# Splitting the first layer's input and the first two weight slabs on ScalarE and VectorE, with GpSimd beginning at the third slab

## The chip, the cores and the metric

The kernel runs on one core of a Trainium2 chip. The metric is the device time of one execution, in microseconds (us). A core has a matrix engine (TensorE, PE in the rows; its weight loads are PEld), VectorE (DVE), ScalarE (ACT), GpSimd (POOL) and SyncE, which here only issues DMAs (SPq). The engines run their own instruction streams and meet at semaphores.

## What is computed

Two layers of a decoder trunk over 528 tokens (16 meta tokens and 512 others) of 1024 channels. The part that matters here is the very start of the first layer: a root mean square norm and the first projection.

```python
def rms_norm(t, g, eps=NORM_EPS):
    y = t32 * lax.rsqrt(jnp.mean(t32 * t32, axis=-1, keepdims=True) + eps)
    return (y * g)
...
    for l in range(DEPTH):
        u = rms_norm(h, norm_mix[l])
        proj = u @ w_in[l]
        glu_in, q, k, v, gates = jnp.split(proj, SPLITS, axis=-1)
        a = glu_in + b_glu[l]
        a = a[..., :C_CONV] * jax.nn.sigmoid(a[..., C_CONV:])
        a = causal_depthwise_conv(a, conv_w[l], conv_b[l])
        ...
        h = h + merged @ w_o[l]
        u = rms_norm(h, norm_mlp[l])
        h = h + jnp.square(jax.nn.relu(u @ w_up[l])) @ w_down[l]
```

The kernel multiplies the input by the gain before the projection and applies the inverse root afterwards, so the projection needs only `h * gain`, while the inverse root needs the sum of the squares of `h` over all channels.

## The kernel before

Channels lie on the 128 partitions: `h` is 8 tiles of 128 x 528. Every float32 product is made of three products of parts: an operand is split into a high part (rounded to the type fp32r) and a low part (the rest), and TensorE adds high x high, high x low and low x high. So the input tile `u[:, 0, i]` is the high part of `h * gain`, `u[:, 1, i]` the low part, and a slab of weights `w_raw` (128 x 2048 float32, 1 MB) becomes `w_hi` and `w_lo`. There are two buffers of each; slabs alternate between them.

The start of layer 0 runs as follows.

SyncE issues the transfers: `h` tiles 0 and 1, slab 0, `h` tiles 2 and 3, 4 and 5, 6 and 7, three small constants (L468, semaphore `in_landed`), slab 1 (L469). The transfer of slab 2 waits until slab 0 has been split (`w_ready`), that of slab 3 until slab 1 has.

GpSimd splits each slab in `split` (L493 to L496): a tiny `tick`, one TENSOR_SCALAR over 128 x 2048 for `w_hi`, four TENSOR_TENSOR over 128 x 512 for `w_lo`, then `w_ready`. From slab 2 on it first waits until TensorE has finished the slab that was in the buffer (`w_used`).

ScalarE and VectorE go through the 8 input tiles in `norm_tile`. ScalarE writes the square into one of two buffers (L828) and the high part (L830). VectorE adds the square to `sumsq` (L1074) and writes the low part (L1075), then raises `u_ready`. ScalarE waits before tile k for the VectorE work on tile k - 2.

TensorE waits for the small constants and for slab 0, then runs the first output tile: 8 input chunks with 6 matmuls of 264 columns each (L588), each chunk waiting for `u_ready`. Between the first and second output tile it sums `sumsq` over partitions (`partition_sums`, L622 and L625). Then come the second tile of slab 0, both tiles of slab 1, and so on; each slab is two output tiles of 48 matmuls. The fourth output tile reuses the PSUM of the second and so waits (`a_free`) for VectorE's L1269, which needs the inverse root: L1244, a square root on ScalarE (L968), the reciprocal L1246, and three instructions of a Newton step (L1081 to L1083).

Order on each engine is the written order; there is no planner around this place.

Of the kernel before, what the change touches and what calls it, by code (L numbers as in the profile page):

```python
# [25 lines left out]
ACT = mybir.ActivationFunctionType  # L26
# [201 lines left out]
def build(nc, x_t, w_slabs, pvecs, rows_in, ident_in, mask_in, identb_in, out, h_spill):  # L228
    ctx = ExitStack()
    with ctx:  # L230
# [8 lines left out]
        def at(name, shape, dt, offset):  # L239
            return nc.alloc_sbuf_tensor_at(name, shape, dt, offset=offset)  # L240
# [11 lines left out]
        down_tmp = at("down_tmp", [P, T], F32, r_x)  # L252
        sumsq = at("sumsq", [P, T], F32, r_x + ROW)
        sq = at("sq", [P, 2, T], F32, r_x + 2 * ROW)

        o_t = at("o_t", [P, NT, T], F32, r_o)
        glu_g = at("glu_g", [P, 2, T], F32, r_o)
# [85 lines left out]
        const_ready = sem("const_ready")  # L343
        h_new = sem("h_new")
        u_hi, u_ready = sem("u_hi"), sem("u_ready")
        ms_ready, sqrt_ready = sem("ms_ready"), sem("sqrt_ready")
        ln_ready = sem("ln_ready")
        glu_sig, glu_out = sem("glu_sig"), sem("glu_out")
# [134 lines left out]
        def _(pool):  # L483
            chain = Count(pool, p_chain)

            def split(b, nth, first=False):

                pool.wait_ge(w_landed[b], 16 * nth + 16)
                if not first:

                    pool.wait_ge(w_used, 2 * nth + (b - 1))

                nc.gpsimd.tensor_tensor(tick[:], ones[:, 0:1], ones[:, 0:1], ALU.mult)  # L493
                chain.link(nc.gpsimd.tensor_scalar(w_hi[:, b, :], w_raw[:, b, :], 1.0, 1.0, ALU.mult, ALU.mult))  # L494
                for c in range(0, SLAB, SLAB // 4):
                    last = nc.gpsimd.tensor_tensor(w_lo[:, b, c:c + SLAB // 4], w_raw[:, b, c:c + SLAB // 4], w_hi[:, b, c:c + SLAB // 4], ALU.subtract)  # L496
                last.then_inc(w_ready, 1)
# [51 lines left out]
                nc.gpsimd.tensor_tensor(t4[:, :, :, H2:HD], x4[:, :, :, 0:H2], mid4(tabs[:, x, 1, :, H2:HD], 4), ALU.mult).then_inc(turned, 1)  # L549

            pool.wait_ge(const_ready, 1)
            for b in range(2):
                split(b, 0, first=True)
            done = 1
            for layer in range(LAYERS):
                s0 = layer * SLABS + S_QKV
# [19 lines left out]
        def _(pe):  # L576
# [183 lines left out]
            for layer in range(LAYERS):  # L760

                a_slabs(layer, 0, A_GLU, N_GLU // 2, u, (u_ready, layer * 2 * NT), full=True,
                        hooks=[lambda: partition_sums(layer, u_ready, (layer * 2 + 1) * NT, sumsq, full=True, cols=True)])

                pe.wait_ge(a_free[0], layer * A_TILES // 2 + NT)
                for stage in range(5):
                    tiles, n = b_tiles(layer), b_before(layer, stage)
                    for step, x, *c in schedule(layer, stage):
                        if step == "tile":
                            what, t = tiles[x]  # L770
                            slab = layer * SLABS + S_QKV + 3 * stage + "vqk".index(what)
                            pe.wait_ge(w_ready, slab + 1)
                            b_tile(layer, n + x, slab % 2, t, c[0])
                        elif step == "gate":
                            early_gate(layer, x, c[0])
                        elif step in ("q", "k"):
                            qk_transposes(layer, x, step, c[0] if c else None)
                        elif step == "s":
                            if (x, *c) == (0, 0):
                                pe.wait_ge(a_free[1], layer * A_TILES // 2 + NT)  # L780
                            scores(layer, x, c[0])
                        elif step == "t":
                            transposes(layer, x, c[0])
                        elif step == "pv":
                            values(layer, x)
                        elif step == "y":
                            y_transposes(layer, x)

                pe.wait_ge(exp_done, (layer + 1) * HEADS * 2 * 3)
                pe.wait_ge(a_free[1], (layer * A_TILES + A_GATE + EARLY_GATES) // 2)  # L790


                channel_sums(layer, ln_ready, layer + 1, [r_inv2[:], conv[:, NT - 1, :]], st_full)

                def last_y():

                    pe.wait_ge(centred, layer * NT + 1)
                    y_transposes(layer, HEADS - 1)
                def squares_summed():

                    for i in range(NT):
                        pe.wait_ge(squared, layer * NT + i + 1)
                        channel_sums(layer, None, 0, [ln_sq[:, i % 4, :]], st_full if i == NT - 1 else sq_used, begins=i == 0, ends=i == NT - 1)
                a_slabs(layer, S_GATE + 4, A_GATE + 8, 1, u, None, hooks=[squares_summed, last_y])
                a_slabs(layer, S_GATE + 6, A_GATE + 12, 1, u, None)
                a_slabs(layer, S_PW, A_PW, 2, cact, (cact_ready, layer * NT))
                a_slabs(layer, S_O, A_O, 2, u, (m_ready, layer * NT))
                for k, (what, g) in enumerate(MLP_ORDER):
                    if what == "up":
                        a_slabs(layer, S_MLP + 4 * k, A_MLP + 8 * k, 2, u2, (u_ready, (layer * 2 + 1) * NT))  # L810
                        if g == 0:
                            partition_sums(layer, u_ready, (layer * 2 + 2) * NT, sumsq)
                    else:
                        a_slabs(layer, S_MLP + 4 * k, A_MLP + 8 * k, 2, hid[g % 2], (hid_ready, (layer * 4 + g) * NT))
# [3 lines left out]
        def _(act):  # L818
# [3 lines left out]
            def norm_tile(i, k, par, layer, gain, dst, full=False):  # L822

                if not (isinstance(k, int) and k < 2):

                    act.wait_ge(u_ready, k - 1)
                lo, n, _ = (0, T, 2) if full else span(layer)
                nc.scalar.activation(sq[:, par, lo:lo + n],  # L828
                                     h[:, ds(i, 1), lo:lo + n].rearrange("p o n -> p (o n)"), ACT.Square)
                nc.scalar.mul(dst[:, 0, ds(i, 1), lo:lo + n].rearrange("p o n -> p (o n)"),  # L830
                              h[:, ds(i, 1), lo:lo + n].rearrange("p o n -> p (o n)"), pvec[:, ds(gain + i, 1)]).then_inc(u_hi, 1)
# [125 lines left out]
            for layer in range(LAYERS):  # L957
                lo, n, k = span(layer)
                if layer == 0:
                    act.dma_start(pvec[:], pvecs[layer]).then_inc(pv_landed, 16)  # L960
                    act.wait_ge(pv_landed, 16)
                    for i in range(NT):
                        act.wait_ge(h_landed[i // 2], 16)
                        norm_tile(i, i, i % 2, 0, V_NMIX, u, full=True)
                if layer == 0:
                    act.dma_start(rows[:], rows_in[layer]).then_inc(rows_landed, 16)
                act.wait_ge(ms_ready, layer + 1)
# [97 lines left out]
        def _(dve):  # L1065
# [167 lines left out]
            for layer in range(LAYERS):  # L1233
# [1 line left out]
                lam_init = 0.8 - 0.6 * math.exp(-0.3 * layer)  # L1235
                dve.wait_ge(pv_landed, 16 * (layer + 1))
                if layer == 0:
                    link(V.memset(sumsq[:], 0.0))
                    for i in range(NT):
                        dve.wait_ge(h_landed[i // 2], 16)  # L1240
                        norm_tile(i, i, i % 2, 0, V_NMIX, u, full=True)

                dve.wait_ge(st_full, layer * 4 + 1)
                announce(dve, V.tensor_scalar(row(r_inv2[:], layer, True), st_ps(layer, True), 1.0 / D, NORM_EPS, ALU.mult, ALU.add), ms_ready, layer + 1)  # L1244
# [292 lines left out]
```

## Time and profile before

| | us |
|---|---|
| median of 3 runs | 1986.39 |
| the runs | 1983.84, 1986.39, 1986.53 |
| the profiled execution | 1983.29 |
| its span in the trace | 1981.5 |
| TensorE busy | 1872.2 (94% of the span) |
| VectorE busy | 1278.1 (65%) |
| GpSimd busy | 1126.7 (57%) |
| ScalarE busy | 559.3 (28%) |

The span begins with the first recorded instruction and ends with the last; 1.8 us lie outside it. TensorE is busy in nearly every slice of the span except the first.

### The profile page before, as it was taken

The page shows a single profiled execution, that of the slowest core. Times are in us where ns is not written, and L with a number is a line of the kernel's source. Part 1 is how long each engine was busy: PE and PEld are TensorE (multiplying, and loading weights), DVE is VectorE, ACT ScalarE, POOL GpSimd, SP SyncE. Part 2 cuts the span into 40 slices and gives each one's busy share as a digit, 9 for nine tenths or more (in the row PEclk, how much of TensorE's full clock was granted, in tenths as well). Part 3 has the DMA queues.
Part 4 walks back from the last instruction along what each step waited for, and adds up shares of the span by engine and source line. Part 5 has one row for each costly group of instructions (what it writes and reads, how often), then busy time and mean ns, then how long its engine had stood idle before and what let it go on. Part 6 is the DMA issues. An engine that isn't in the chain of part 4 may idle for free. (4 is left out here: it accounts for less than half of the span.)

```text
span 1981.5 us, 34343 instructions
## 1 busy us (share of the span) xinstructions
PE 1872.2 (94%) x12950; PEld 1693.5 (85%) x12950; DVE 1278.1 (65%) x1823; ACT 559.3 (28%) x1721; POOL 1126.7 (57%) x1124
## 2 busy tenths in 40 slices
PE   5999999899899999999999988898998999999999
PEld 5998788788899999999989987787766778888887
DVE  7997877978564433334569979779885654434443
ACT  3124665534312210111111344555334122110100
POOL 5667443423666676666656564334236677676764
PEclk9999999999999999999999998999999999999999
DMA  4221111011222222222332211110113222322222
GB/s 148 104 86 62 40 50 43 30 57 43 108 93 98 86 85 86 103 89 99 107 107 85 86 65 44 43 43 22 64 43 109 105 85 85 106 85 106 86 92 78
DMA packets 23870, 156.37 MB, mean 79 GB/s; under 512 B 2896, under 2 KB 3280, under 8 KB 6096
## 3 DMA queue, kind: packets, MB, share of 16 engines
q1 hardware_dynamic: 21744, 147.01, 20.9%
q10 hardware_dynamic: 2016, 7.86, 1.1%
q8 instruction: 74, 1.21, 0.2%
q14 instruction: 36, 0.29, 0.0%
HBM read 150.59 MB, written 4.26 MB: 78 GB/s over the span
## 5 line engine op out<-in xcount | busy, mean ns | idle before, releaser
L588 PE MATMUL psum<-u,w_hi 128*128 128x264 f32 (+1 forms) x4480 | 919.3, 317 | 51.8 <-DVE sg L1227 22.6
L588 PEld LDWEIGHTS psum<-u,w_hi 128*128 128x128 f32 x4480 | 682.3, 190 | 110.4 <-issue 24.5
L496 POOL TENSOR_TENSOR w_lo<-w_raw,w_hi 128x512 fp32r<-128x512 f32 x448 | 643.7, 1466 | 9.3
L588 PE MATMUL psum<-u,w_lo 128*128 128x264 f32 (+1 forms) x2240 | 568.9, 314 | 0.0
L588 PEld LDWEIGHTS psum<-u,w_lo 128*128 128x128 f32 x2240 | 370.8, 190 | 25.6
L648 PE MATMUL psum<-w_hi,u 128*128 128x256 f32 (+1 forms) x1856 | 348.5, 289 | 0.0
L493 POOL TENSOR_TENSOR tick<-ones 128x1 f32<-128x1 f32 x112 | 25.5, 228 | 538.6 <-PE psum L588 531.7
L441 DVE SCALAR_TENSOR_TENSOR psum<-xg,pvec,psum 128x512 f32<-128x512 f32 x440 | 299.5, 750 | 4.1 <-DVE xg L1271 2.2
L648 PEld LDWEIGHTS psum<-w_hi,u 128*128 128x128 f32 (+1 forms) x1856 | 272.2, 177 | 8.3 <-issue 0.4
L648 PE MATMUL psum<-w_lo,u 128*128 128x256 f32 (+1 forms) x928 | 264.3, 285 | 0.0
L503 POOL TENSOR_TENSOR w_lo<-w_raw,w_hi 128x128 fp32r<-128x128 f32 x384 | 180.5, 510 | 92.0 <-ACT w_hi L871 92.0
L494 POOL TENSOR_SCALAR w_hi<-w_raw 128x2048 fp32r<-128x2048 f32 x112 | 214.8, 1917 | 0.0
L1447 DVE TENSOR_TENSOR relu<-relu 128x528 f32<-128x528 f32 (+1 forms) x64 | 80.7, 1261 | 199.8 <-ACT u L1045 102.2
L1043 ACT ACTIVATE relu<-psum 128x528 f32<-128x528 f32 (+1 forms) x64 | 38.7, 604 | 461.8 <-PE psum L588 461.8
L648 PEld LDWEIGHTS psum<-w_lo,u 128*128 128x128 f32 (+1 forms) x928 | 163.8, 176 | 4.1
L588 PE MATMUL psum<-hid_b,w_hi 128*128 128x264 f32 (+1 forms) x768 | 163.8, 322 | 0.0
L1466 DVE TENSOR_TENSOR down_tmp<-psum,r_inv 128x528 f32<-128x528 f32 (+1 forms) x64 | 44.8, 700 | 174.5 <-PE psum L588 172.9
L548 POOL TENSOR_TENSOR rtmp<-raw,tabs 128x640 f32<-128x640 f32 x16 | 26.0, 1622 | 190.5 <-ACT squares L862 188.5
L588 PEld LDWEIGHTS psum<-hid_b,w_hi 128*128 128x128 f32 x768 | 118.9, 188 | 11.6
L1467 DVE TENSOR_TENSOR h<-h,down_tmp 128x528 f32 (+1 forms) x64 | 97.1, 1517 | 10.3 <-DVE down_tmp L1466 10.3
L588 PE MATMUL psum<-hid_b,w_lo 128*128 128x264 f32 (+1 forms) x384 | 102.4, 321 | 0.0
L889 ACT ACTIVATE e<-psum,nb,q_scale 128x272 f32<-128x272 f32 (+4 forms) x144 | 83.9, 587 | 44.8 <-DVE nb L1152 44.8
(169 smaller groups left out, 2083.5 us busy)
## 6 DMA issues: line engine op xcount, KB each, us to landing
w_raw<-w_slabs SPq DMA_DIRECT2D x136, 1024.0 KB, 4.8
h<-x_t SPq DMA_DIRECT2D x4, 528.0 KB, 7.3
h<-x_t ACTq DMA_DIRECT2D x1, 2112.0 KB, 8.3
h_spill<-h ACTq DMA_DIRECT2D x8, 264.0 KB, 2.4
h<-h_spill ACTq DMA_DIRECT2D x1, 2112.0 KB, 8.5
out<-h SPq DMA_DIRECT2D x8, 256.0 KB, 2.0
rows<-rows ACTq DMA_DIRECT2D x2, 512.0 KB, 4.6
pvec<-pvecs ACTq DMA_DIRECT2D x2, 156.5 KB, 2.9
```

What stands on the lines that cost most here:

```text
L441: return nc.vector.scalar_tensor_tensor(out=done if ends else acc, in0=x, scalar=w, in1=done if begins else acc, op0=ALU.mult, op1=ALU.add)
L494: chain.link(nc.gpsimd.tensor_scalar(w_hi[:, b, :], w_raw[:, b, :], 1.0, 1.0, ALU.mult, ALU.mult))
L496: last = nc.gpsimd.tensor_tensor(w_lo[:, b, c:c + SLAB // 4], w_raw[:, b, c:c + SLAB // 4], w_hi[:, b, c:c + SLAB // 4], ALU.subtract)
L503: last = nc.gpsimd.tensor_tensor(w_lo[:, b, c:c + P], w_raw[:, b, c:c + P], w_hi[:, b, c:c + P], ALU.subtract)
L548: nc.gpsimd.tensor_tensor(t4[:, :, :, 0:H2], x4[:, :, :, H2:HD], mid4(tabs[:, x, 1, :, 0:H2], 4), ALU.mult)
L588: last = nc.tensor.matmul(psum[:, 2 * slot + j, 0:n], w[:, b, cut], src[:, part, kc, at0:at0 + n], start=(kc == 0 and m == 0), stop=(kc == ...
L648: last = nc.tensor.matmul(psum[0:tn, n % 2, 0:2 * P], u[:, part, kc, t0:t0 + tn], w[:, b, kc * 2 * P:(kc + 1) * 2 * P], start=(kc == 0 and ...
L889: ins = nc.scalar.activation(e[0:tn, c, E_OFF[i]:E_OFF[i] + w], psum[0:tn, banks[c], S_AT[i]:S_AT[i] + w], ACT.Exp, bias=nb[0:tn, c, i:i + ...
L1043: nc.scalar.activation(row(relu[:, j, :], layer), a_ps(layer, j), ACT.Relu).then_inc(a_free[j], 1)
L1447: link(V.tensor_tensor(relu2[:, lo:lo + n], relu[:, j, lo:lo + n], relu[:, j, lo:lo + n], ALU.mult))
L1466: announce(dve, V.tensor_tensor(row(down_tmp[:], layer), a_ps(layer, j), row(r_inv2[:], layer), ALU.mult), a_free[j], a_read(layer, A_MLP ...
L1467: ins = V.tensor_tensor(rown(h, ch, layer), rown(h, ch, layer), row(down_tmp[:], layer), ALU.add)
```

## The change

In layer 0 only, the work at the start is written out anew.

- ScalarE writes the high parts of tiles 0 and 1, then the high part of slab 0 (one copy over 128 x 2048), then the high parts of tiles 2 to 7, then all eight squares, each into a buffer of its own (the first into `sumsq` itself), then the high part of slab 1.
- VectorE writes the low parts of tiles 0 and 1, the low part of slab 0 in one TENSOR_TENSOR over 128 x 2048 (raising `w_ready`), the low parts of tiles 2 to 7, then seven additions of squares, then the low part of slab 1. The zeroing of `sumsq` is gone.
- `partition_sums` of layer 0 waits for the new semaphore `x_summed` after the seventh addition, in place of the last `u_ready`.
- GpSimd waits for both slabs' `w_ready` and begins with slab 2.

```diff
+        sq_all = at("sq_all", [P, NT - 2, T], F32, r_x + 2 * ROW)
+        sq_of = [sumsq[:], down_tmp[:]] + [sq_all[:, i, :] for i in range(NT - 2)]
...
+        x_sq, x_summed, w_first = sem("x_sq"), sem("x_summed"), sem("w_first")
...
             pool.wait_ge(const_ready, 1)
-            for b in range(2):
-                split(b, 0, first=True)
+
+            pool.wait_ge(w_ready, 2)
...
-                        hooks=[lambda: partition_sums(layer, u_ready, (layer * 2 + 1) * NT, sumsq, full=True, cols=True)])
+                        hooks=[lambda: partition_sums(layer, *((u_ready, (layer * 2 + 1) * NT) if layer else (x_summed, 1)), sumsq, full=True, cols=True)])
...
                     for i in range(NT):
+                        if i == 2:
+                            act.wait_ge(w_landed[0], 16)
+                            nc.scalar.copy(w_hi[:, 0, :], w_raw[:, 0, :]).then_inc(w_first, 1)
                         act.wait_ge(h_landed[i // 2], 16)
-                        norm_tile(i, i, i % 2, 0, V_NMIX, u, full=True)
+                        nc.scalar.mul(u[:, 0, i, :], h[:, i, :], pvec[:, V_NMIX + i:V_NMIX + i + 1]).then_inc(u_hi, 1)
+                    for i in range(NT):
+                        nc.scalar.activation(sq_of[i], h[:, i, :], ACT.Square).then_inc(x_sq, 1)
+                    act.wait_ge(w_landed[1], 16)
+                    nc.scalar.copy(w_hi[:, 1, :], w_raw[:, 1, :]).then_inc(w_first, 1)
...
-                    link(V.memset(sumsq[:], 0.0))
+                    def first_low(b):
+
+                        dve.wait_ge(w_landed[b], 16)
+                        dve.wait_ge(w_first, b + 1)
+                        V.tensor_tensor(w_lo[:, b, :], w_raw[:, b, :], w_hi[:, b, :], ALU.subtract).then_inc(w_ready, 1)
+
                     for i in range(NT):
+                        if i == 2:
+                            first_low(0)
                         dve.wait_ge(h_landed[i // 2], 16)
-                        norm_tile(i, i, i % 2, 0, V_NMIX, u, full=True)
+                        dve.wait_ge(u_hi, i + 1)
+                        V.scalar_tensor_tensor(out=u[:, 1, i, :], in0=h[:, i, :], scalar=pvec[:, V_NMIX + i:V_NMIX + i + 1], in1=u[:, 0, i, :],
+                                               op0=ALU.mult, op1=ALU.subtract).then_inc(u_ready, 1)
+                    for i in range(1, NT):
+                        dve.wait_ge(x_sq, i + 1)
+                        ins = V.tensor_tensor(sumsq[:], sumsq[:], sq_of[i], ALU.add)
+                        if i < NT - 1:
+                            link(ins)
+                        else:
+                            announce(dve, ins, x_summed, 1)
+                    first_low(1)
```

VectorE before, from its zeroing of `sumsq` on: the pair of instructions of a tile comes eight times, then the inverse root.

```order
L1238 MEMSET sumsq 128x528
L1074 TENSOR_TENSOR sumsq<-sumsq,sq 128x528
L1075 SCALAR_TENSOR_TENSOR u<-h,pvec,u 128x528
L1074 TENSOR_TENSOR sumsq<-sumsq,sq 128x528
L1075 SCALAR_TENSOR_TENSOR u<-h,pvec,u 128x528
```

VectorE now, at the same place, up to the inverse root (`r_inv_93` is the same tile under another name).

```order
L1259 SCALAR_TENSOR_TENSOR u<-h,pvec,u 128x528 x2
L1252 TENSOR_TENSOR w_lo<-w_raw,w_hi 128x2048
L1259 SCALAR_TENSOR_TENSOR u<-h,pvec,u 128x528 x6
L1263 TENSOR_TENSOR sumsq<-sumsq,down_tmp 128x528
L1263 TENSOR_TENSOR sumsq<-sumsq,sq_all 128x528 x6
L1252 TENSOR_TENSOR w_lo<-w_raw,w_hi 128x2048
L1271 TENSOR_SCALAR r_inv_93<-psum 128x528
```

The low parts moved ahead of the additions, and two slab subtractions came in, one between low parts 1 and 2 and one ahead of the inverse root.

ScalarE now, from its first instruction of the kernel's work to the square root; before, squares (L828) and high parts (L830) alternated tile by tile, with no CAST.

```order
L970 ACT_TABLE_LOAD
L970 ACTIVATE u<-h,pvec 128x528 x2
L968 CAST w_hi<-w_raw 128x2048
L970 ACTIVATE u<-h,pvec 128x528 x6
L972 ACTIVATE sumsq<-h 128x528
L972 ACTIVATE down_tmp<-h 128x528
L972 ACTIVATE sq_all<-h 128x528 x6
L974 CAST w_hi<-w_raw 128x2048
L976 DMA rows<-rows 128x1024
```

The squares moved behind all high parts, and the two slab casts stand ahead of high part 2 and ahead of the transfer of `rows`.

## Rows read from the trace of the kernel before

**Rows 1.** The page: busy us, share and instruction count of each engine
```profile
PE 1872.2 (94%) x12950; PEld 1693.5 (85%) x12950; DVE 1278.1 (65%) x1823; ACT 559.3 (28%) x1721; POOL 1126.7 (57%) x1124
```

**Rows 2.** Waits of TensorE in 0 to 60 us: total, times, longest
```profile
PE psum L588 <- POOL w_lo L496: 16.7, 1, 16.7
PE psum L588 <- DVE u L1075: 3.8, 3, 2.4
```

**Rows 3.** Timeline of the start: start us, duration us, engine, instruction, [idle before <-releaser]
```profile
5.68 0.64 ACT L828 ACTIVATE sq<-h 128x528 f32<-128x528 f32 x1
6.23 0.72 ACT L830 ACTIVATE u<-h,pvec 128x528 fp32r<-128x528 f32 x1
6.86 0.63 ACT L828 ACTIVATE sq<-h 128x528 f32<-128x528 f32 x1
...
7.43 0.41 POOL L493 TENSOR_TENSOR tick<-ones 128x1 f32<-128x1 f32 x1 [6.97 <-DMA w_raw<-w_slabs]
...
9.78 6.67 POOL L496 TENSOR_TENSOR w_lo<-w_raw,w_hi 128x512 fp32r<-128x512 f32 x4
10.29 1.66 DVE L1074 TENSOR_TENSOR sumsq<-sumsq,sq 128x528 f32<-128x528 f32 x1
...
16.71 1.22 PE L588 MATMUL psum<-u,w_hi 128*128 128x264 f32 x4 [16.71 <-POOL w_lo L496]
...
18.16 1.08 PE L588 MATMUL psum<-u,w_hi 128*128 128x264 f32 x4
...
24.64 1.25 PE L588 MATMUL psum<-u,w_hi 128*128 128x264 f32 x4 [2.40 <-DVE u L1075]
```

**Rows 4.** The same timeline, where GpSimd has done both slabs
```profile
26.32 0.77 DVE L1075 SCALAR_TENSOR_TENSOR u<-h,pvec,u 128x528 fp32r<-128x528 f32 x1
27.12 0.71 DVE L1074 TENSOR_TENSOR sumsq<-sumsq,sq 128x528 f32<-128x528 f32 x1
...
31.07 1.05 PE L622 MATMUL psum<-sumsq,ones 128*128 128x264 f32 x4
...
33.09 0.73 PE L588 MATMUL psum<-u,w_hi 128*128 128x264 f32 x4
```

**Rows 5.** Landing of the first transfers (h, the constants): us from issue to landing
```profile
L466 SPq DMA_DIRECT2D h<-x_t x4: 391/444/647, 0.8 to 2.8; - x4
...
DMA to landing us min/median/max: 3.6/7.3/8.4
```

**Rows 6.** Last constant's issue (timeline); landing of the constants, then of slab 1
```profile
4.34 0.47 SPq L468 DMA_DIRECT2D identb<-identb  x1
...
DMA to landing us min/median/max: 7.5/7.7/8.0
...
DMA to landing us min/median/max: 9.3/9.3/9.3
```

**Rows 7.** ScalarE's casts of whole slabs (by line); a VectorE TENSOR_TENSOR of 128 columns (timeline)
```profile
L871 ACT CAST w_hi<-w_raw x24: 1891/1924/1938, 135.5 to 1376.1; 128x2048 fp32r<-128x2048 f32 x24
...
59.99 0.29 DVE L1285 TENSOR_TENSOR rows<-rows 128x128 f32<-128x128 f32 x1
```

**Rows 8.** Stretches: length, busy us (count) by engine, granted clock, DMA share, GB/s
```profile
24.60:27.10 2.50, 1.69 (x6) 1.38 (x6) 2.44 (x2) 1.27 (x2) 1.11 (x1) 0.50 0.15 26
...
33.10:38.90 5.80, 5.80 (x49) 5.80 (x49) 4.73 (x3) 0.65 (x1) 0.00 (x0) 1.00 0.02 3
```

**Rows 9.** TensorE alone in a later stretch with a dip of its clock
```profile
180.00:186.00 6.00, 5.99 (x50) 0.72 0.52 175
```

**Rows 10.** Timeline, from the inverse root on, up to slab 2
```profile
33.35 0.71 DVE L1244 TENSOR_SCALAR r_inv<-psum 128x528 f32<-128x528 f32 x1 [3.17 <-PE psum L625]
...
39.81 2.46 DVE L1083 SCALAR_TENSOR_TENSOR r_inv<-glu_a,r_inv 128x528 f32<-128x528 f32 x1
41.80 5.84 POOL L496 TENSOR_TENSOR w_lo<-w_raw,w_hi 128x512 fp32r<-128x512 f32 x4
...
43.31 0.70 DVE L1269 TENSOR_TENSOR glu_a<-psum,r_inv 128x528 f32<-128x528 f32 x1
```

## The prediction

> **What bounds the kernel now.** I read the page first: TensorE is busy for 1872.2 of 1981.5 us, no other engine for more than 65% [rows 1]. So whatever is won must be a stretch in which TensorE stands still or runs slowly. Second, the waits of TensorE over the first 60 us: it waits 16.7 us for GpSimd's low part of slab 0, and 3.8 us in three pieces for VectorE's low parts of the input [rows 2]. Third, the timeline of that start. Slab 0 has landed when GpSimd's `tick` starts at 7.43; then come `tick` and `w_hi` until 9.78 and 6.67 for `w_lo`, and TensorE starts at 16.71 [rows 3]. From there VectorE holds it up: its TENSOR_TENSOR over 128 x 528 takes 1.66 us while GpSimd works [rows 3], and 0.71 (0.77 for the low part) once GpSimd is through [rows 4]. The first output tile, eight chunks of input, therefore lasts from 16.71 to the partition sums at 31.07, 14.4 us. With full clock and nothing to wait for, a tile takes 5.8 us: that many matmuls (49 where a tile has 48) fill the stretch from 33.10 to 38.90 [rows 8]. The second output tile starts at 33.09 [rows 4], and from there I see no more waits of TensorE until after 60 us, since these are all that the view lists [rows 2]. So **the time at which the second output tile starts** is what the change can move: 33.09 now.
>
> **The change part by part.**
>
> *Slab 0 on ScalarE.* ScalarE starts its first instruction at 5.68, the next 0.55 later, and one high part takes 0.63 until the next start [rows 3]. Two high parts end at about 7.0. The cast then waits for slab 0, landed at about 7.4 as GpSimd's start shows [rows 3]. ScalarE's cast of a slab of this very shape takes 1.92 [rows 7]: done at 9.35. GpSimd needed until 9.78.
>
> *Slab 0 on VectorE.* No row before has VectorE subtracting 128 x 2048 elements. Lower bound and value taken: a TENSOR_TENSOR from SBUF takes 0.29 at 128 columns [rows 7] and 0.71 at 528 [rows 4], that is 1.05 ns a column; 0.71 + 1520 x 1.05 ns = 2.3 us. Upper bound from the same engine's nearest rows: four instructions of 0.77 [rows 4], 3.1 us. It is one instruction with one start, so I take 2.3. `w_ready` at 9.4 + 2.3 = 11.7.
>
> *TensorE's start.* It also waits for the three constants. The last is issued at 4.34 and lands 7.5 us later, at 11.8 [rows 6]. This wait was covered by GpSimd before and now arrives together with `w_ready`. Start at about 11.9, **4.8 us earlier**.
>
> *Input.* The last two tiles of `h` are issued at 2.8 and land 8.4 later, at 11.2 [rows 5]; ScalarE comes to them at 9.2 + 4 x 0.63 = 11.7, so the landing costs nothing. High part 7 is begun by 12.4. VectorE goes on at 11.7 with six low parts of 0.78 each from start to start: all done at 16.4. GpSimd does nothing in this time, so I take the undisturbed 0.77.
>
> *Squares.* ScalarE's eight squares run from 13.0, 0.55 apart [rows 3], to 17.5. VectorE's seven additions start at 16.4, later than the squares need, and take 7 x 0.75 (0.71 and the wait of each on the one ahead): `x_summed` at 21.7. The removed zeroing and the eighth addition are in that count.
>
> *The first output tile.* From 11.9 on, TensorE starts with chunks of 1.45 us (16.71 to 18.16) [rows 3]. With two or three chunks at that pace it needs 5.8 + 1.6 = 7.5 us and is done by 19.5; with four, 20.7. Either is before 21.7. So TensorE's start is not what counts any more: **VectorE's chain of additions ends last**, and the partition sums begin at 21.8 in place of 31.07. This is 9.3 us earlier.
>
> *The clock.* TensorE then pauses from about 19.5 to 21.8. Before, it paused 2.40 us ahead of the chunk at 24.64, and behind that pause the granted clock is 0.50, which is 1.2 of 2.4 GHz [rows 3, 8]. A pause of 2.3 us behind a short burst is of the same kind, so I expect one dip. Its price is in a later dip: a granted 0.72 over 6.0 us is 0.28 x 2 x 6.0 = 3.4 us at half rate [rows 9], which costs half of that, 1.7 us. A dip twice as long would cost 3.4, none 0. I take 1.7.
>
> The Trainium skill has a rule that speaks for a better result. "TensorE: Matmul & The Clock Gate", in the section on why this matters for your kernels, warns only of pauses longer than the one that I forecast; by it the full clock would stay and the 1.7 us would not be lost. The 2.40 us pause of this trace, followed by the half rate, differs from it.
>
> *Slab 1.* ScalarE casts it from 17.4 to 19.3; it was issued behind the last constant, at 4.9, and landed 9.3 later, at 14.2 [rows 6]. VectorE subtracts behind the additions, 21.7 to 24.1. TensorE wants it after the second output tile, at 23.8 + 5.8 = 29.6 or later: hidden by that tile. What is queued behind it on VectorE is the inverse root, which wants the partition sums at 21.8 + 2.1 = 23.9: 0.2 late. Before, this chain ran from 33.35 to the end of L1269 at 44.01 [rows 10], 10.7 us, of which 1.7 are the collision of L1083 with GpSimd's `w_hi` of slab 2 (2.46 us, up to just past the start of its `w_lo`; 0.71 without). The fourth output tile wanted it at 33.09 + 2 x 5.8 = 44.7. So the old slack was 0.7 us, and the new one is 24.1 + 10.7 = 34.8 against 23.8 + 11.6 = 35.4, 0.6 us, more if the clock dips. Free, but barely.
>
> *GpSimd.* Its new wait for `w_ready` 2 ends at 24.1, and behind it is the old wait for `w_used`, at 29.6 or later: nothing. It then needs some 8.5 us for slab 2 as before (from the end of the second tile, 33.09 + 5.8 = 38.9, to 41.80 + 5.84 = 47.6) [rows 4, 10], and TensorE wants it 11.6 us on. The transfers of slabs 2 and 3 hang on `w_ready` and the transfer of `rows` on ScalarE's queue, and all three are issued earlier than now. All hidden.
>
> **Sum.** 9.3 - 1.7 = 7.6 us less in the span and, as all behind the second output tile hangs on TensorE and moves with it, in the time: 1983.3 - 7.6 = 1975.7 for an execution like the profiled one. That one lies 3.1 below the median, which itself is at the upper of two clusters. The mean of the three runs is 1985.6, and I forecast **1978.0** from it. About 0.2%, 4 us, is what a measurement of this kernel can tell from no change.
>
> **The rivals.**
>
> *The clock stays full* through the pause, because the first tile runs on later than I think or the pause is short enough. For it: a slow start of the tile leaves a pause of 1.1 us, half of the one that did harm. Gain 9.3: 1976.3.
>
> *Part of it is given back.* The subtraction takes 3.1, which moves `x_summed` by 0.8 and the inverse root by 1.6 and uses up the slack; or one more VectorE instruction is caught by GpSimd's slab 2 (1.7); or the dips later in the kernel, each 1.7, fall one or two more often. With two such prices on top of the sum the gain is 7.6 - 3.4 = 4.2: 1981.4; with three it is 2.5, which is no change: 1983.1.
>
> *The change does not do what it says*: the start is tied to a landing. Against it: even slab 1's landing at 14.2 as TensorE's start would let the tile end at 21.7. Small; if transfers landed 5 us later all would be later by 5, a gain of 2.6: 1983.0.
>
> *Slower: VectorE becomes the bound through the slab subtractions.* Call the price of one p. `x_summed` is at 19.4 + p, the inverse root begins at 19.4 + 2p, and the fourth output tile can start 10.7 later, at 30.1 + 2p. Before it started at 44.7, so this loses from p = 7.3 on. GpSimd's price for the same work is 6.67 [rows 3]; with p = 8.5 the loss would be 2.4 from this alone, and with the dip 4.1: 1989.7. Against it: VectorE's rows of the same kind cost a third of GpSimd's per column.
>
> **How the numbers follow.** Forecast 0.50, clock full 0.22, part given back 0.18 (0.05 of it as no change), tied to a landing 0.04, slower 0.03, something else 0.03. Low end: the gain 9.3 from the lower cluster (1983.3) is 1974.0; high end: the gain 4.2 from the upper one is 1982.3. That gives 1973.8 to 1982.5. Faster by over 0.2%: 0.88; within: 0.08; slower: 0.04.
>
> **What would show it.** TensorE's first matmul at about 11.9 and the partition sums at 21.8, released by VectorE's L1263; the `w_lo` subtraction of VectorE at 2.3; low parts at 0.77; no GpSimd work before 29; a granted clock of 0.5 for some 3.4 us around 22 to 26; TensorE without a wait for L1296 (the old L1269) at the fourth output tile. Wrong are the sum if the second output tile starts later than 26, and the reasoning on the rest if that tile starts 7 us earlier but the end of the span does not.

## The result, and the profile after

| | before | changed |
|---|---|---|
| median of 6 runs each, us | 1986.10 | 1974.54 |
| the runs, from to, us | 1982.85 to 1987.34 | 1973.40 to 1976.94 |
| ratio of the runs, 95% interval | | 0.9946 (0.9934 to 0.9959) |
| the profiled execution, us | 1983.29 | 1976.94 |
| its span, us | 1981.5 | 1975.2 |

The change makes the kernel faster by 0.54%, between 0.41% and 0.66%: 8 to 13 us. The medians are 11.6 us apart, the two profiled executions only 6.35; the profiled execution of the changed kernel was the slowest of its six. The leads below trace 9.9 us of this to the start; the rest is inside the interval and is not explained.

The waits of TensorE in the first 60 us, after: they answer to [rows 2]. Columns: total, times, longest.

```profile
PE psum L591 <- DMA identb<-identb: 12.2, 1, 12.2
PE psum L625 <- DVE sumsq L1263: 0.4, 1, 0.4
```

GpSimd's 16.7 us are gone. What ends TensorE's first wait is not even a weight any more, but the last small constant. The waits of 3.8 us for the low parts are gone too.

The timeline of the start, after (start, duration, engine, instruction, idle before and its releaser); it answers to [rows 3, 4].

```profile
7.60 1.90 ACT L968 CAST w_hi<-w_raw 128x2048 fp32r<-128x2048 f32 x1 [0.19 <-DMA w_raw<-w_slabs]
...
9.60 2.29 DVE L1252 TENSOR_TENSOR w_lo<-w_raw,w_hi 128x2048 fp32r<-128x2048 f32 x1 [1.23 <-ACT w_hi L968]
11.81 4.16 DVE L1259 SCALAR_TENSOR_TENSOR u<-h,pvec,u 128x528 fp32r<-128x528 f32 x6
...
12.24 1.22 PE L591 MATMUL psum<-u,w_hi 128*128 128x264 f32 x4 [12.24 <-DMA identb<-identb]
...
15.88 0.70 DVE L1263 TENSOR_TENSOR sumsq<-sumsq,down_tmp 128x528 f32<-128x528 f32 x1
...
16.62 4.42 DVE L1263 TENSOR_TENSOR sumsq<-sumsq,sq_all 128x528 f32<-128x528 f32 x6
...
17.44 1.89 ACT L974 CAST w_hi<-w_raw 128x2048 fp32r<-128x2048 f32 x1
...
20.31 0.40 PE L591 MATMUL psum<-u,w_lo 128*128 128x264 f32 x2
21.08 2.29 DVE L1252 TENSOR_TENSOR w_lo<-w_raw,w_hi 128x2048 fp32r<-128x2048 f32 x1
...
21.10 1.16 PE L625 MATMUL psum<-sumsq,ones 128*128 128x264 f32 x4 [0.39 <-DVE sumsq L1263]
...
23.24 0.73 PE L591 MATMUL psum<-u,w_hi 128*128 128x264 f32 x4
```

VectorE has no gap of note from 9.60 to the sums: slab, six low parts, seven additions. The first output tile runs from 12.24 to 20.7. The sums start at 21.10, at once behind the last addition, and the second output tile at 23.24 in place of 33.09 [rows 4], **9.85 us earlier**. The clock stays full behind the pause. A stretch across it (length, busy us and count by engine, granted clock, DMA share, GB/s):

```profile
20.00:30.00 10.00, 9.61 (x75) 8.97 (x75) 9.01 (x8) 1.28 (x2) 0.59 (x2) 1.00 0.32 107
```

The inverse root and GpSimd's first slab, after; they answer to [rows 10].

```profile
23.41 0.71 DVE L1271 TENSOR_SCALAR r_inv<-psum 128x528 f32<-128x528 f32 x1
...
29.41 0.49 POOL L496 TENSOR_TENSOR tick<-ones 128x1 f32<-128x1 f32 x1 [28.95 <-PE psum L591]
29.85 1.92 POOL L497 TENSOR_SCALAR w_hi<-w_raw 128x2048 fp32r<-128x2048 f32 x1
29.87 2.46 DVE L1093 SCALAR_TENSOR_TENSOR r_inv<-glu_a,r_inv 128x528 f32<-128x528 f32 x1
...
33.36 0.70 DVE L1296 TENSOR_TENSOR glu_a<-psum,r_inv 128x528 f32<-128x528 f32 x1
```

The same collision of L1093 with GpSimd's `w_hi` is there, 2.46 us, and the chain ends at 34.06, while the fourth output tile is due at 23.24 + 11.7 = 34.9. TensorE does not wait for it.

**Where the lead goes later.** Both kernels issue the same 12950 matmuls in the same order, so the start of the same matmul can be compared between two traces. The lead of the changed kernel, in us, at times of the kernel before:

```
time of before     38    170    186    338    406    586    672    1045   1228   1398   1966
changed          9.87   9.87   9.40   9.39   7.28   8.68   7.64   5.31   4.95   5.90   6.34
changed again   10.09  10.09   9.04   8.11   8.13   8.13   8.19   8.22   8.21   9.17   9.03
before again    -1.20  -1.20  -1.82  -2.66  -2.71  -1.94  -1.95  -2.02  -2.09  -1.17  -1.14
```

The lead from the start is held without loss up to the attention of layer 0. What is lost behind it is not lost at the same places in a second execution of the same kernel, and the kernel before drifts against itself as well (third line, and there the start itself differed by 1.2). So the 3.5 of the 9.9 us that are missing in the one profiled pair are no fixed price of the change: the second pair lost 1.05. The largest step, 2.3 us between 672 and 1045, stands where the granted clock is at half for 10.2 us in the first trace (from 1007.4) and for 6.8 us in the second (from 1005.1).

### The profile page after: what moved, and what is told of

It is laid out like the page before. It is cut to its first block and busy times, and to the rows that moved or that the text cites. A ratio compares the mean times of both kernels' runs of the same rounds, so it can differ in the third digit from the quotient of the medians.

```text
span 1975.2 us, 34338 instructions
## 1 busy us (share of the span) xinstructions
PE 1873.1 (95%) x12950; PEld 1695.6 (86%) x12950; DVE 1266.7 (64%) x1823; ACT 562.4 (28%) x1723; POOL 1107.6 (56%) x1112
## 5 line engine op out<-in xcount | busy, mean ns | idle before, releaser
L499 POOL TENSOR_TENSOR w_lo<-w_raw,w_hi 128x512 fp32r<-128x512 f32 x440 | 629.7, 1461 | 9.2
L591 PEld LDWEIGHTS psum<-u,w_lo 128*128 128x128 f32 x2240 | 371.5, 191 | 25.6
```

The costliest lines, as they stand in the source:

```text
L591: last = nc.tensor.matmul(psum[:, 2 * slot + j, 0:n], w[:, b, cut], src[:, part, kc, at0:at0 + n], start=(kc == 0 and m == 0), stop=(kc == ...
```

## The experiments

The numbers ahead of each verdict are the median time in us, the ratio to the kernel before on the same chip with its interval, and the lead over the first trace of the kernel before at the matmul that started there at 38 us, where the second output tile is nearly through. The changed kernel has 9.87 there. Three kernels have two traces each, and their leads differ by 0.2 (the changed kernel), 1.2 (the kernel before) and 1.6 us (only the input reordered), so a difference of under 2 us between two leads counts only where the lines of the traces show its cause. Diffs are against the changed kernel unless said.

### Only the slabs moved

```diff
-                        nc.scalar.mul(u[:, 0, i, :], h[:, i, :], pvec[:, V_NMIX + i:V_NMIX + i + 1]).then_inc(u_hi, 1)
-                    for i in range(NT):
-                        nc.scalar.activation(sq_of[i], h[:, i, :], ACT.Square).then_inc(x_sq, 1)
+                        norm_tile(i, i, i % 2, 0, V_NMIX, u, full=True)
...
-                        V.scalar_tensor_tensor(out=u[:, 1, i, :], in0=h[:, i, :], scalar=pvec[:, V_NMIX + i:V_NMIX + i + 1], in1=u[:, 0, i, :],
-                                               op0=ALU.mult, op1=ALU.subtract).then_inc(u_ready, 1)
-                    for i in range(1, NT):
-                        dve.wait_ge(x_sq, i + 1)
-                        ins = V.tensor_tensor(sumsq[:], sumsq[:], sq_of[i], ALU.add)
+                        norm_tile(i, i, i % 2, 0, V_NMIX, u, full=True)
```

The zeroing of `sumsq` is back as well, and the sums wait for the last `u_ready` again.

> Only the slabs move to ScalarE and VectorE; the input keeps its old order, square and high part in turn, addition and low part in turn. Theory (taking the two slabs off GpSimd gives nearly all): the low parts and additions run undisturbed at 0.77 and 0.71, the last low part ends at 21.8, the sums start after one more chunk at 22.5, the second output tile starts at 24.6, which is 8.5 us ahead of the kernel before, and the time is 8 to 9 us lower. Rival (the new order of squares and additions is what gives it): the second output tile starts later than 29 and the time falls by less than 4.

Measured: 1976.74, 0.9956 (0.9942 to 0.9969), lead 8.25. Its timeline:

```profile
13.03 1.22 PE L591 MATMUL psum<-u,w_hi 128*128 128x264 f32 x4 [13.03 <-DVE w_lo L1251]
...
21.16 0.77 DVE L1083 SCALAR_TENSOR_TENSOR u<-h,pvec,u 128x528 fp32r<-128x528 f32 x1
21.98 0.76 PE L591 MATMUL psum<-u,w_hi 128*128 128x264 f32 x4 [0.55 <-DVE u L1083]
...
22.82 1.05 PE L625 MATMUL psum<-sumsq,ones 128*128 128x264 f32 x4
```

As expected to within 0.3 us in the trace (the median is 9.3 us lower, against 8 to 9 expected): 8.25 of the 9.87 us come from taking the slabs off GpSimd. The remaining 1.6 us are the order of the input work: with additions and low parts in turn the last chunk of the first tile waits for the last low part (21.98), and the sums come behind it at 22.82 in place of 21.10. The times of this kernel and of the changed one don't tell them apart.

### Only the input's order changed

```diff
-            pool.wait_ge(w_ready, 2)
+            for b in range(2):
+                split(b, 0, first=True)
...
-                            nc.scalar.copy(w_hi[:, 0, :], w_raw[:, 0, :]).then_inc(w_first, 1)
...
-                    nc.scalar.copy(w_hi[:, 1, :], w_raw[:, 1, :]).then_inc(w_first, 1)
...
-                            first_low(0)
...
-                    first_low(1)
```

> Only the order of the input work changes; GpSimd still splits both first slabs. Theory: VectorE's low parts and additions still run against GpSimd at 1.66 each until 25.7, x_summed comes at about 29, the second output tile starts at about 31, 2 us ahead of the kernel before, and a clock dip behind the longer pause takes most of it: time within 2.5 us of before. Rival (the new order gives it): second output tile at 27 or earlier, time 5 us or more lower.

Measured: 1992.25, 1.003 (1.0018 to 1.0041), lead -1.03. **Slower than before.** Its timeline:

```profile
9.71 8.57 DVE L1253 SCALAR_TENSOR_TENSOR u<-h,pvec,u 128x528 fp32r<-128x528 f32 x6 [1.35 <-ACT u L968]
...
12.43 1.77 DVE L1253 SCALAR_TENSOR_TENSOR u<-h,pvec,u 128x528 fp32r<-128x528 f32 x1
...
17.29 1.22 PE L592 MATMUL psum<-u,w_hi 128*128 128x264 f32 x4 [17.29 <-POOL w_lo L499]
...
20.12 6.72 POOL L499 TENSOR_TENSOR w_lo<-w_raw,w_hi 128x512 fp32r<-128x512 f32 x4
20.63 8.26 DVE L1257 TENSOR_TENSOR sumsq<-sumsq,sq_all 128x528 f32<-128x528 f32 x6
...
25.52 0.40 PE L592 MATMUL psum<-u,w_lo 128*128 128x264 f32 x2
27.44 0.71 DVE L1257 TENSOR_TENSOR sumsq<-sumsq,sq_all 128x528 f32<-128x528 f32 x1
28.94 1.35 PE L626 MATMUL psum<-sumsq,ones 128*128 128x264 f32 x4 [3.02 <-DVE sumsq L1257]
30.22 2.01 PE L629 MATMUL psum<-ones,sumsq 128*16 128x2 f32 x10
32.09 1.23 PE L592 MATMUL psum<-u,w_hi 128*128 128x264 f32 x4
```

(The two single VectorE lines at 12.43 and 27.44 are inside the groups that start at 9.71 and 20.63.) The theory held for the start. While GpSimd subtracts, a low part takes 1.77 us, the next one starting 1.7 behind it, and an addition 1.65 to 1.68 (1.66 expected); once GpSimd's last instruction has ended, at 26.84, an addition takes 0.71. The sums start at 28.94, as forecast. The new order alone wins nothing. TensorE pauses 3.02 us ahead of the sums, and behind the pause a row of four matmuls takes 1.23 in place of 0.73: half rate, which turns a lead of 1.0 at the second tile's start (33.09 - 32.09) into -1.0. The median is 6.2 us above that of the kernel before, where the expectation had 2.5 at most. The rest is seen in the trace much later; that has a run of its own.

### The same kernel again

> The kernel with only the input reordered, for a second trace. In the first one it was 1.0 us behind the kernel before at 200 us and lost another 5 us between 1550 and 1590, where VectorE's collisions with GpSimd in layer 1's pointwise stage took up to 2.4 us each. Theory A (the shift of the start puts this stage into another alignment of the two engines, every time): the loss at 1550 to 1590 repeats. Theory B (chance): it is absent and the time is within 2.5 us of before.

Measured: 1991.17 in a single run, lead -2.62 at the start, 1.6 us behind the first trace. TensorE's pause ahead of the sums is 3.58 us here, and the clock is at half for 10 us from 28.8 on, in place of 6.8. The loss far behind repeats: between 1568 and 1588 us of its span the lead falls from -0.8 to -7.9; in the first trace from -5.2 to -12.3 at the same matmuls. TensorE's waits from 1500 to 1660 in the second trace, and below it the same view of the kernel before:

```profile
PE psum L592 <- DVE u L1445: 5.2, 2, 4.5
```

```profile
PE psum L588 <- DVE u L1425: 1.5, 1, 1.5
```

VectorE there loses against GpSimd in a pattern that the other kernels don't show, in both traces with the same durations, for example:

```profile
1549.94 2.34 DVE L1445 TENSOR_TENSOR u<-m_tmp,u 128x512 f32 x1 [0.98 <-ACT u L1031]
...
1561.25 2.43 DVE L1443 TENSOR_TENSOR m_tmp<-m_tmp,g_tmp 128x512 f32<-128x512 f32 x1
```

The other nine traces have no VectorE instruction of over 2 us from 1530 to 1600. So it is not chance (theory B falls). The shift of the start is not enough for it either: just ahead of the loss this trace is 0.8 us behind the first trace of the kernel before, the second trace of that kernel 1.3 and the kernel below with a busy GpSimd 2.2, both without the loss. TensorE's longest wait, 4.5 us, ends at 1584.03, and the granted clock is at half from 1581.8 for 6.8 us, so a part of the 7 us is the clock. Why just this program enters that stage in another alignment of the two engines stays open.

### GpSimd busy for nobody

```diff
+            pool.wait_ge(h_landed[0], 16)
+            for k in range(10):
+                chain.link(nc.gpsimd.tensor_tensor(raw[:, k % 2, 0:2, :].rearrange("p t c -> p (t c)"), h[:, 0, 0:512], h[:, 1, 0:512], ALU.subtract))
             pool.wait_ge(w_ready, 2)
```

> The changed kernel with ten GpSimd TENSOR_TENSOR of 128 x 512 (of no use, from h into an unused tile) from the landing of h on, so that GpSimd is busy until about 20 as before but nobody waits for it. Theory A (two SBUF inputs on VectorE and GpSimd's reads exclude each other, so half of the gain is that VectorE is undisturbed): low parts take 1.66, the slab subtraction over 3, the sums start at 25 to 28 and the lead over the kernel before falls from 9.9 to 3 to 6 us. Rival B (only the latency of GpSimd's own split counted): VectorE's instructions keep 0.7, the lead stays 9.9.

Measured: 1985.64, 0.9999 (0.9990 to 1.0009), lead -1.13. **All of the gain is gone**, though TensorE starts at 13.13 and nothing waits for GpSimd. Its timeline:

```profile
4.65 18.02 POOL L558 TENSOR_TENSOR raw<-h 128x512 f32<-128x512 f32 x10 [4.19 <-DMA h<-x_t]
...
9.49 3.38 DVE L1255 TENSOR_TENSOR w_lo<-w_raw,w_hi 128x2048 fp32r<-128x2048 f32 x1
12.80 10.44 DVE L1262 SCALAR_TENSOR_TENSOR u<-h,pvec,u 128x528 fp32r<-128x528 f32 x6
...
28.36 2.13 PE L628 MATMUL psum<-sumsq,ones 128*128 128x264 f32 x4 [4.08 <-DVE sumsq L1266]
```

Six low parts take 10.44 us against 4.16 and the slab 3.38 against 2.29. GpSimd's ten instructions, the last of which ends at 22.67, take 1.80 each in the mean, and from 14 us on both engines start one every 1.73 us: the two take turns. The additions, behind GpSimd's last one, take their 0.74 again. The sums start 7.3 us later than in the changed kernel, and another 3.7 go to half rate behind a pause of 4.08. Theory A is right in kind and was sized too small: the chain alone leaves a lead of 2.6 where 3 to 6 was expected, and the clock was left out. The Trainium skill says the same of this pair of engines ("SBUF — State Buffer", section "Who interferes with whom"): a VectorE instruction with two SBUF inputs contends with a GpSimd instruction that reads SBUF, and contention there is an exclusive lock. The trace agrees: 1.74 us from start to start for a low part that takes 0.69 alone.

### VectorE's chain made longer

```diff
+                    V.tensor_tensor(raw[:, 0, :, :].rearrange("p t c -> p (t c)")[:, 0:SLAB // 2], h[:, 0:2, :].rearrange("p a t -> p (a t)")[:, 0:SLAB // 2], h[:, 2:4, :].rearrange("p a t -> p (a t)")[:, 0:SLAB // 2], ALU.subtract)
+                    V.tensor_tensor(raw[:, 1, :, :].rearrange("p t c -> p (t c)")[:, 0:SLAB // 2], h[:, 0:2, :].rearrange("p a t -> p (a t)")[:, 0:SLAB // 2], h[:, 2:4, :].rearrange("p a t -> p (a t)")[:, 0:SLAB // 2], ALU.subtract)
                     for i in range(1, NT):
                         dve.wait_ge(x_sq, i + 1)
```

> The changed kernel with two more VectorE subtractions of 128 x 1024 (of no use, into an unused tile) between the last low part and the additions, 1.2 us each. Theory (VectorE's additions set the start of the sums): sums start 2.4 less the 0.0 of slack later, at 23.5, the fourth output tile waits some 2 us more for the inverse root, TensorE's pause grows from 0.4 to 2.8 us. Whether the clock dips behind this pause tells the forecast's term from its rival: with a dip the second output tile is 5.7 us ahead of the kernel before, without one 7.4. Rival (TensorE's first tile sets it): sums still at 21.1.

Measured: 1978.73, 0.9961 (0.9948 to 0.9974), lead 4.65.

```profile
20.40 0.40 PE L591 MATMUL psum<-u,w_lo 128*128 128x264 f32 x2
...
23.22 1.16 PE L625 MATMUL psum<-sumsq,ones 128*128 128x264 f32 x4 [2.42 <-DVE sumsq L1265]
24.31 1.72 PE L628 MATMUL psum<-ones,sumsq 128*16 128x2 f32 x10
25.89 1.23 PE L591 MATMUL psum<-u,w_hi 128*128 128x264 f32 x4
```

The sums move by 2.1 us (the two instructions take 2.3 from start to start, and this trace's chain began 0.1 earlier), so VectorE's additions do set them. And behind a pause of 2.42 us the clock goes to half rate. Stretches of this kernel (length, busy us and count by engine, granted clock, DMA share, GB/s):

```profile
20.70:23.50 2.80, 0.38 (x2) 0.28 (x2) 2.66 (x5) 0.00 (x0) 0.00 (x0) 1.00 0.00 0
...
25.50:32.00 6.50, 6.50 (x32) 6.50 (x33) 5.09 (x4) 0.64 (x1) 0.00 (x0) 0.53 0.45 164
```

The dip came, as the forecast's term supposed for such a pause, and it took 3.1 us on top of the shift (9.87 - 2.1 - 4.65), not 1.7: the half rate held for more than 6 us. The fourth output tile did not wait for the inverse root, against the expectation: the tiles ahead of it had become slower as well, and L1093 did not meet GpSimd this time (0.71 us in place of 2.46).

### Slab 0 in two halves

```diff
-                        if i == 2:
+                        if i in (2, 4):
+                            x = slice((i // 2 - 1) * (SLAB // 2), (i // 2) * (SLAB // 2))
                             act.wait_ge(w_landed[0], 16)
-                            nc.scalar.copy(w_hi[:, 0, :], w_raw[:, 0, :]).then_inc(w_first, 1)
+                            nc.scalar.copy(w_hi[:, 0, x], w_raw[:, 0, x]).then_inc(w_first, 1)
...
+                            V.tensor_tensor(w_lo[:, 0, x], w_raw[:, 0, x], w_hi[:, 0, x], ALU.subtract).then_inc(w_half if i == 2 else w_ready, 1)
...
-            pe.wait_ge(in_landed, 48)
...
+                pe.wait_ge(in_landed, 48)
                 for stage in range(5):
```

TensorE begins on `w_half` and waits for `w_ready` ahead of the fifth chunk; the wait for the constants has moved from its start to the attention's stages, which use them first.

> The changed kernel with slab 0 split in two halves on ScalarE and VectorE (the second half between tiles 3 and 4 of the input), TensorE beginning on the first half and not waiting for the constants until they are used. Theory (VectorE's chain sets the sums, TensorE's start has slack): TensorE starts at about 10 in place of 12.2, but the sums only 0.6 us earlier, at 20.5, by the idle time in front of VectorE's slab subtraction that is filled; the time changes by less than 1 us. Rival (TensorE's start sets the end): the sums and all behind them come 2.2 us earlier.

Measured: 1975.13, 0.9950 (0.9936 to 0.9963), lead 7.58: with TensorE starting 2.2 us earlier and VectorE's chain done 0.8 earlier, it is **2.3 us behind** the changed kernel by the end of the second tile.

```profile
10.03 1.22 PE L594 MATMUL psum<-u,w_hi 128*128 128x264 f32 x4 [10.03 <-DVE w_lo L1267]
...
20.33 1.40 PE L632 MATMUL psum<-sumsq,ones 128*128 128x264 f32 x4 [2.33 <-DVE sumsq L1274]
21.66 2.02 PE L635 MATMUL psum<-ones,sumsq 128*16 128x2 f32 x10
23.53 1.23 PE L594 MATMUL psum<-u,w_hi 128*128 128x264 f32 x4
```

A stretch of it (columns as above):

```profile
21.20:27.90 6.70, 6.70 (x32) 6.23 (x31) 4.82 (x3) 0.64 (x1) 0.00 (x0) 0.50 0.50 159
```

Neither theory nor rival had this. The sums come 0.8 us earlier, as the theory said, so TensorE's start does not set them. But the earlier start only made a pause of 2.33 us, and the sums (3.2 us in place of 2.1) and the tile behind them run at half rate.

### Halves, with the late start kept

The diff is against the kernel with the halves.

```diff
             pe.wait_ge(const_ready, 1)
+            pe.wait_ge(in_landed, 48)
...
-                pe.wait_ge(in_landed, 48)
```

> The kernel with slab 0 in halves, but TensorE waits for the constants again and so starts at 12.1 instead of 10.0. Theory (the earlier start only lengthened the pause ahead of the sums to 2.3 us, behind which the clock ran at half rate and took 2.3 us): the first tile ends at about 20, the pause is under 0.7 us, the sums start at 20.4 at full clock, and the second output tile is 10.3 to 10.6 us ahead of the kernel before, more than the changed kernel's 9.9, though TensorE starts 2 us later than without the wait. Rival (the half rate there is chance, or hangs on something else than the pause): the lead is 7.6 again or less.

Measured: 1971.66, 0.9934 (0.9921 to 0.9947), lead 10.47.

```profile
12.39 1.22 PE L594 MATMUL psum<-u,w_hi 128*128 128x264 f32 x4 [12.39 <-DMA identb<-identb]
...
20.50 1.16 PE L632 MATMUL psum<-sumsq,ones 128*128 128x264 f32 x4 [0.19 <-DVE sumsq L1274]
...
22.64 0.73 PE L594 MATMUL psum<-u,w_hi 128*128 128x264 f32 x4
```

TensorE starts 2.4 us later than in the kernel above and is 2.9 us ahead of it by the end of the second tile. The one edit is the wait, and the pause is 0.19 in place of 2.33, with full clock behind it. Each of the two kernels has one trace, and their times don't tell them apart (0.9921 to 0.9947 against 0.9936 to 0.9963); what carries the 2.9 us is that the lines show the half rate in the one and not in the other. Of all kernels this one has the largest lead, 0.4 and 0.6 us more than the two traces of the changed one. That it beats the changed kernel is not shown: the intervals overlap (0.9934 to 0.9959 there), and a lead of 0.4 us from one trace is too near to the 0.2 by which the changed kernel's own two traces differ. That it beats the kernel before is shown by time and trace.

### The two kernels again

> The changed kernel again, for a second trace. Theory (the 3.5 us that the profiled execution lost between 170 and 1260 us are half-rate stretches of the clock that fall otherwise in each execution): the start repeats to 0.1 us, the lead over the kernel before at 100 us is 9.9 again, but the later losses lie at other places or are absent. Rival (the earlier start itself costs it in the attention stages): the same losses at the same places.

Measured: 1975.78, 0.9955 (0.9942 to 0.9969), lead 10.09. Sums at 20.87 behind a pause of 1.33 us, at full clock. The start repeats to 0.2 us, and the late losses are at other places, as the leads in the section on the result show: the rival, the same losses at the same places, falls. The pause is longer than in the first trace since the first tile was through at 19.5: two of its chunks and a part of the third ran slowly, not four. That the late losses of the changed kernel are half-rate stretches is shown for the largest one alone.

> The kernel before again, for a second trace: its start repeats to 0.1 us, its half-rate stretches between 300 and 1500 us differ in number or length from the first trace by one to three, each worth 1.7 us.

Measured in a single run: 1984.41.

```profile
17.14 1.22 PE L588 MATMUL psum<-u,w_hi 128*128 128x264 f32 x4 [17.14 <-POOL w_lo L496]
...
25.06 0.86 PE L588 MATMUL psum<-u,w_hi 128*128 128x264 f32 x4 [2.19 <-DVE u L1075]
...
30.66 1.25 PE L588 MATMUL psum<-u,w_hi 128*128 128x264 f32 x4
```

The start did not repeat to 0.1 us, as I had expected, but was 1.2 us late at the second tile. 0.4 of it is there at TensorE's first matmul; most of the rest is the last chunk, which still ran at half rate here. Behind the pause of 2.19 us the granted clock is at half from 25.6 to 32.3. Between 300 and 1500 us the clock is at half 12 times in this trace and 15 times in the first, 61 us in all against 72. That is three fewer, as the expectation allowed, and over this part the second trace gains 3.8 us on the first (the lead goes from -4.2 to -0.4), against 5 if all of the 10 us had cost half. Between 100 and 300 it is the other way round: the second trace has two such stretches of 6.8 us, the first one of 3.4, and the second loses 3.0 us on the first. So much of the drift between two traces of one kernel goes with such stretches, though no run here tells what places them.

## Why the prediction was right

The forecast was 1978.0 with a range of 1973.8 to 1982.5; measured were 1974.54. The direction, the place and the chain that ends last were right. The size was too small, and one term is the main reason.

- *What can be won.* The second output tile's start moved from 33.09 to 23.24; up to 170 us all behind it moved with it. Right. With GpSimd made busy again the whole gain went, 7.3 us of it by VectorE's chain and 3.7 by the clock, so the rows of VectorE's instructions at 1.66 against 0.71 and 0.77 were the ones to build on.
- *Slab 0.* Cast 1.90 (forecast 1.92), subtraction 2.29 (2.3, taken at the low end of 2.3 to 3.1). Right: the cost per column from two shorter rows of the same engine carried to one four times as long.
- *TensorE's start.* 12.24 (11.9), released by the last constant as forecast.
- *Input and squares.* Sums at 21.10 (21.8). The six low parts take 4.16 us, 0.69 each, not 0.78: one alone takes 0.77 as before, but the next starts 0.69 behind it, where in the old pairs of addition and low part the next start was 0.74 to 0.80 behind. The additions, each of which needs the one ahead, came at 0.74. This is 0.5 of the 0.7 us.
- *The first tile.* It ended at 20.7, not at 19.5: four of its chunks ran at the slow pace, not two or three. The text had both ends, and the sum was right to rest on VectorE, but the clock term rested on the early one. (5.8 + 1.6 is 7.4 and not 7.5; nothing hangs on it.)
- *The clock.* This is the step that failed: 1.7 us for a dip that did not come. The pause was 0.39 us (1.33 in the second trace) instead of 2.3, as the first tile ended 1.2 us later and the sums came 0.7 earlier. Where a pause of 2.33 or 2.42 us was made, the dip did come, and took 3.1 us each time instead of 1.7 (in the kernel with the halves the 2.3 us that it fell behind and the 0.8 by which its sums were earlier). So the supposed effect was real, its occurrence wrong, and its price too small. The price came from a later dip of 3.4 us, while the dip behind the very pause of 2.40 us that the prediction leans on lasts longer in the same trace:

```profile
24.60:30.20 5.60, 4.75 (x18) 4.14 (x18) 5.39 (x6) 3.82 (x5) 1.11 (x1) 0.50 0.56 198
```

By the rule of the Trainium skill ("TensorE: Matmul & The Clock Gate", section "Why this matters for your kernels") that warns of pauses over about 3 us, the gain would have been put at 9.3, close to the 9.9 measured, but not for its reason: the pause was short. On pauses of 2.19, 2.33, 2.40 and 2.42 us, each followed by half rate, the runs differ from it.
- *Slab 1 and the inverse root.* The slack forecast at 0.6 was 0.8. The chain from L1271 to L1296 took 10.65 as before. (GpSimd's slab 2 before is 8.7 us by the prediction's own rows, not 8.5.)
- *The sum.* 9.9 us in place of 7.6. From the mean of the first three runs, 1985.6, this is 1975.7; the medians of six runs say 11.6 with an interval of 8 to 13, which holds it. So 2.3 us of the forecast's error of 3.5 are the sum's. The rest no trace accounts for; it is within the scatter of the runs. And the measured median lies only 0.7 above the low end of the range.
- *The rivals.* "The clock stays full" (1976.3) is what happened. The slower one would have needed a subtraction of 7.3 us. "Part of it is given back" appeared in the profiled pair (3.5 us), but the second trace of the changed kernel lost only 1.

## What to carry to other kernels

Where two engines shut each other out, work taken off the one also gives the other its full speed back, even where nobody waited for the first: here GpSimd work of no use cost 7.3 us on VectorE's chain. At a start, find the chain that ends last before making something else earlier. An earlier start of TensorE that only lengthened its pause lost time by the clock here, and holding it back until its operands flowed won 2.9 us, in one trace of each. For edits worth a few us, compare the start of the same instruction in two traces, since the time itself scatters by some 5 us; the start scatters too, by 0.2 to 1.6 us here, so take a second trace before a small difference is believed.

## What the runs showed that I had not expected

- A pause of TensorE of 2.33 or 2.42 us behind a first tile of some 8 to 9 us was followed by half rate (1.2 in place of 2.4 GHz) and cost about 3 us; pauses of 0.19, 0.39 and 1.33 at the same place cost nothing beyond themselves. All seven traces in which TensorE, once started, paused for 2.19 us or more in the first 30 us (up to 4.08) have the half rate, from a moment in the pause or at most 1.6 us behind its end. What lies between 1.33 and 2.19 was not tried.
- Ten useless GpSimd instructions (18 us) at a place where GpSimd is otherwise idle cost 11 us of TensorE's lead: 7.3 on VectorE's chain and 3.7 by the clock.
- In the kernel with only the input reordered VectorE and GpSimd meet otherwise 1540 us later, and this cost 7 us there in both of its traces. Its cause is open.
